# Low halves of the weight tiles: one GpSimd subtraction of 1024 columns per tile in place of two of 512

## What is computed

```
m, conv_state, s_new = token_mix(rms_norm(x), ...)      # Conformer conv group + GLA group
x = x + m
x = x + cross_attn(rms_norm(x), mk, mv, w_q, w_o)        # 4 heads, 256 memory tokens
h = rms_norm(x)
x = x + square(relu(h @ w_up)) @ w_down                  # width 4096
y = rms_norm(x)
```

## Time and profile before

| what | value |
|---|---|
| median of 3 runs | 1675.45 us (1673.5 to 1676.83) |
| profiled execution: its own time | 1673.81 us |
| profiled execution: span from first to last instruction | 1672.1 us |
| PE busy | 1511.8 us, 90% of the span |
| DVE busy | 701.2 us, 42% |
| POOL busy | 534.4 us, 32%, of which low parts 371.2 us |
| ACT busy | 461.2 us, 28% |
| mean granted TensorE clock | 0.947 |

### The profile page before, as it was taken

The page is one execution under the profiler, slowest core; times in us unless marked ns, Lnnn a source line. Parts: engine busy times, 40 slices in busy tenths (PEclk is TensorE's granted clock), DMA queues, the critical chain, the costliest instruction groups (busy, mean ns, idle before and its releaser), DMA issues.

```text
span 1672.1 us, 22350 instructions
## 1 busy us (share of the span) xinstructions
PE 1511.8 (90%) x9454; PEld 1458.9 (87%) x9454; DVE 701.2 (42%) x659; ACT 461.2 (28%) x544; POOL 534.4 (32%) x352
## 2 busy tenths in 40 slices
PE   5987777786889899997899999999999999999995
PEld 4887767776877899996699999999999999999994
DVE  6499989957861533546323221112210221112123
ACT  6422215133342323234222321112210221122211
POOL 6247759724551122210012222212212222212220
PEclk9998878988998899999899999999999999999997
DMA  6221501100020424114711111111111111111102
GB/s 228 83 71 57 62 33 57 45 26 26 14 63 29 164 94 184 51 50 152 278 38 38 51 50 51 38 51 38 51 49 50 38 50 50 50 38 50 44 31 101
DMA packets 45530, 114.00 MB, mean 68 GB/s; under 512 B 7688, under 2 KB 20248, under 8 KB 44320
## 3 DMA queue, kind: packets, MB, share of 16 engines
q1 hardware_dynamic: 43568, 104.19, 19.0%
q10 hardware_dynamic: 1904, 8.98, 1.3%
HBM read 100.85 MB, written 12.30 MB: 68 GB/s over the span
## 4 chain that ended last, share of the span: by engine, by line
PE 68%; DVE 19%; issue 6%; POOL 3%; ACT 3%; DMA 1%; DVEq 0%; SPq 0%; ACTq 0%; POOLq 0%
PE ps L978 63%; DVE conv_y L1423 10%; DVE qz L1447 1%; PE m L1049 1%; PE m L1209 1%; DVE acc L1447 1%; PE ps L1243 1%; POOL w_split L537 1%; PE m L997 1%; DVE acc L1413 1%; DMA cache_b<-in_cache_v 1%; DVE sc_t L1458 1%; DVE x_res L1821 1%; DVE tmp L1436 0%; POOL a_op L582 0%
## 5 line engine op out<-in xcount | busy, mean ns | idle before, releaser
L978 PE MATMUL ps<-a_op,w_split 128*128 128x344 f32 x4968 | 817.0, 327 | 50.8 <-DVE tmp L1491 18.7
L978 PEld LDWEIGHTS ps<-a_op,w_split 128*128 128x128 f32 x4968 | 805.6, 194 | 55.2 <-DVE tmp L1491 19.8
L537 POOL TENSOR_TENSOR w_split<-w_raw,w_split 128x512 fp32r<-128x512 f32 x250 | 371.2, 1505 | 1024.7 <-ACT w_split L624 1024.7
L978 PE MATMUL ps<-b_op,w_split 128*128 128x344 f32 x2880 | 454.6, 319 | 0.0
L978 PEld LDWEIGHTS ps<-b_op,w_split 128*128 128x128 f32 x2880 | 452.3, 188 | 0.8 <-issue 0.4
L624 ACT ACTIVATE w_split<-w_raw 128x1024 fp32r<-128x1024 f32 x125 | 131.3, 1050 | 407.3 <-PE ps L978 399.0
L1423 DVE SCALAR_TENSOR_TENSOR conv_y<-conv_in,par,conv_y 128x1024 f32<-128x1024 f32 x90 | 187.0, 2078 | 2.6
L1792 DVE SCALAR_TENSOR_TENSOR tmp<-ps,rstd 128x1032 f32<-128x1032 f32 x32 | 39.5, 1233 | 215.1 <-PE ps L978 203.2
L1802 DVE TENSOR_TENSOR x_res<-x_res,ps 128x1032 f32 x24 | 29.5, 1229 | 230.8 <-PE ps L978 230.8
L932 ACT ACTIVATE tmp<-tmp 128x1032 f32<-128x1032 f32 x32 | 34.1, 1066 | 259.1 <-DVE tmp L1792 259.1
L1632 DVE TENSOR_TENSOR x_res<-x_res,ps 128x1032 f32<-128x1032 f32 x24 | 29.5, 1229 | 166.7 <-PE ps L978 166.7
(11 more groups left out here) (205 smaller groups left out, 952.0 us busy)
## 6 DMA issues: line engine op xcount, KB each, us to landing
w_raw<-in_wt SPq DMA_DIRECT2D x125, 512.0 KB, 3.5
cache_b<-in_cache_v SPq DMA_DIRECT2D x8, 1024.0 KB, 7.3
x_in<-in_x ACTq DMA_DIRECT2D x4, 1032.0 KB, 8.1
x_spill<-x_res SPq DMA_DIRECT2D x8, 516.0 KB, 2.6
out_y<-x_res ACTq DMA_DIRECT2D x8, 516.0 KB, 3.0
cache_a<-in_cache_k SPq DMA_DIRECT2D x2, 2048.0 KB, 11.4
cache_b<-in_cache_k SPq DMA_DIRECT2D x2, 2048.0 KB, 10.4
x_res<-in_x SPq DMA_DIRECT2D x1, 3096.0 KB, 12.3
```

The lines of the kernel that those rows point to most:

```text
L537: gp.tensor_tensor(w_split[:, slot, 1, part, :], w_raw[:, slot, part, :], w_split[:, slot, 0, part, :].bitcast(F32), ALU.subtract).then_in ...
L978: last = pe.matmul(ps[:, b, 0:w], w_split[:, slot, wp, k, :], src[:, k, xp, c0:c0 + w], start=(k == 0 and j == 0), stop=(k == KT - 1 and j ...
```

## The change

POOL's low part of a tile is made by one instruction over all 8 blocks. It adds 2 to `w_low_done` when it ends, so that every count that others wait for (PE at block 0 and block 4, SP before the next load) stays as it was. PE's program isn't changed: its wait at block 0 for 2t + 1 is now met only when the whole low part is there.

```diff
@@ -532,10 +532,8 @@
             def lo(t, slot):
 
                 gp.wait_ge(w_high_done, t + 1)
-                for k in (0, KT // 2):
-                    part = slice(k, k + KT // 2)
-                    gp.tensor_tensor(w_split[:, slot, 1, part, :], w_raw[:, slot, part, :],
-                                     w_split[:, slot, 0, part, :].bitcast(F32), ALU.subtract).then_inc(w_low_done, 1)
+                gp.tensor_tensor(w_split[:, slot, 1, :, :], w_raw[:, slot, :, :],
+                                 w_split[:, slot, 0, :, :].bitcast(F32), ALU.subtract).then_inc(w_low_done, 2)
```

## The result

The changed kernel takes 1684.0 us (median of 5 runs, 1681.42 to 1685.25), the one before 1675.45. The ratio is 1.0052 with a 95% interval of 1.0037 to 1.0066: slower by 8.55 us by the medians. The forecast was slower, 1681.3 us.

The account below looks back on a forecast made before the run. PE was taken as the bound on average, DVE as the pace in the convolution. Terms 0.8 + 2.5 + 1.2 + 1.05 + 0.3 = +5.85 us on the median 1675.45 gave 1681.3 us, range 1674.5 to 1687.

Parts of the forecast that it names:

- One instruction of 2.34 us, the loads 0.19 earlier: POOL's low part: 2.34 us in place of 2.52, so SP's loads come 0.19 us earlier or more.
- Tiles 40 to 124 cost nothing: Feed-forward tiles and those before from 40: later first halves stay covered by the tile before, no cost.
- Tile 39, +1.05: PE starts tile 39 on its first half; waiting for the whole costs +1.05 us, bounds 0.9 to 1.2.
- Tiles 8, 10, 12, 20 covered (0 to +0.8): Convolution in-tiles starting later but ending before DVE reads them: counted as nothing, 0 to +0.8 us.
- The start, +0.8 (-0.7 to +1.9): Start-up: tile 0 starts 1.07 us later, 0.3 taken back through tile 5's earlier load: +0.8 us.
- The levels, +1.2: GLA levels, tiles 34 to 37: DVE's operands wait one longer POOL instruction, +1.2 us, 0 to +2.9.
- Attention, +0.3: DVE's copy of 8 columns at 751.97 us waits for the whole low part: +0.3 us, 0 to +1.1.
- The convolution, +2.5 (-4.3 to +4.6): Convolution stage: 12 disturbed low parts cost DVE's taps 0.20 us each, +2.4, plus +0.1 for tile 10.
- DVE is the pace there: Convolution stage, 76 to 332 us: DVE, busy 240 of 256 us, sets the pace rather than PE.
- nothing to measure: Rival: DVE's turns cost the same and the start gives back its 1.07; +1.5 us, 1677; chance 0.25.
- faster: Rival: DVE loses only POOL's own time, 0.19 less per low part; -3.95 us, 1671.5; chance 0.07.
- The clock: Rival: new idle times before tiles 8, 10, 39 lower PE's clock; +9 us, 1684.5, or 1686.7; chance 0.08.

Follow-up runs that it names:

- e1: Kernel before with one low subtraction per tile only for tiles 40 to 124: ratio 0.9993, -1.2 us.
- e3: Kernel before with one low subtraction only for tiles 0, 2, 3, 4, 8, 10, 12, 20 and 39: ratio 1.0009, +1.5 us.
- e6: Changed kernel with DVE's twelve short operations of the sample tokens' convolution moved behind the last tap: 1684.08 us, ratio 1.0059.
- e8: Kernel before with one low subtraction only for tiles 1, 5, 6, 7, 9, 11 and 32 to 38: ratio 1.0010, +1.7 us.
- e2: Kernel before with one low subtraction only for tiles 13 to 19 and 21 to 31: ratio 1.0037, +6.2 us.
- e4: Kernel before with POOL's tap additions split into two of 512 columns, low parts still in halves: ratio 0.9975, -4.2 us.
- f3: Kernel before with low parts in quarters of 256 columns for tiles 9 to 31, tap additions whole: ratio 0.9963, -6.2 us.
- f2: Kernel before without POOL's 30 tap additions, low parts whole for tiles 13 to 19 and 21 to 31: 1628.86 us, +5.9 over the same in halves.
- f4: Kernel before with low parts in quarters for tiles 9 to 38, whole from tile 40, tap additions in quarters of 256: ratio 0.9958, -7.0 us.

## Why the prediction was right, and where its size was off

The range and the sign held, and the sum came within 2.7 us of the medians, in part by luck: the convolution was priced too low, and the clock gave time back at tiles 37 and 53, where the sum had nothing. By its own steps:
- **One instruction of 2.34 us, the loads 0.19 earlier.** Right: 2.342 us, 125 instructions.
- **Tiles 40 to 124 cost nothing.** Right: but for tile 53 the distance between the traces is constant, and e1 is -1.2 us with an interval that holds 0.
- **Tile 39, +1.05.** Right: +1.15, at full clock, and it stays up to tile 52. At tile 53 the three traces with tile 39 whole are 1.3 us or more faster than any other, which the forecast didn't see.
- **Tiles 8, 10, 12, 20 covered (0 to +0.8).** Not borne out: e3's trace has +3.0 us between tiles 7 and 31, through the wait in front of tile 16. Tile 12 comes 4.0 us late there, of which 1.1 is from the start. DVE reads tile 12 out of PSUM 1.8 us later than before and tile 14 4.1 us later, so the lateness had reached DVE, which the step took as untouched.
- **The start, +0.8 (-0.7 to +1.9).** -0.97 in the changed kernel's profile, +1.1 in e3's and +0.8 in e6's. The waits went as told (the load's wait went and PE's took its place). The size can't be read from these: the kernels that are the same up to tile 8 differ by 3 us there, 2 of them by the clock at tile 5, which the term left out.
- **The levels, +1.2.** 1.6 us came between tiles 31 and 36, in the changed kernel's trace and in e8's. What the term left out is tile 37, where 1.8 us come back in both. So e8's +1.7 us (0.2 to 3.3 by its interval) doesn't measure this term.
- **Attention, +0.3.** It can't be told from nothing. From the end of tile 52 to the start of tile 53 PE takes 81.26 us, 80.62 before and 80.34 in e1; the other traces lie between 80.4 and 81.1.
- **The convolution, +2.5 (-4.3 to +4.6): the term that was mis-sized.** The step was "12 x 0.20", one tap more or less in a turn. The taps' own sum did what it said: 187.0 to 189.3 us, +2.3. But the stage grew by 13.1 us in that pair of traces, and e2, with 18 of its tiles whole, measures +6.2 us (+4.0 to +8.4 by its interval). Two things were left out. One is DVE's other operations, those of few columns above all, which now wait longer for POOL: +8.1 us in that trace. The other is the order in DVE's queue: a fixed number of taps stands in front of each PSUM read, and each lets one POOL instruction through, of whatever length. The longer that is, the more of POOL's work comes to stand in front of the read, where PE waits for it, and the less behind it, where DVE has time to spare. In the two places read above a mean over both sides (0.20) hides a loss of about 2 us in front, and the gain behind goes into DVE's wait for PE. That POOL's instruction size is the cause is shown by e2, e4 and f3; how the loss divides between these two ways is argued from the traces and not shown.
- **"DVE is the pace there"** was true on the average, 240 of 256 us, but in the places read above DVE and PE bound each other in turn. There, waits inside DVE count in front of the read only.

Of the rivals, "nothing to measure" and "faster" are out by the interval, the latter by the earlier trace rows's own pattern. The clock did not fall behind tiles 8, 10 and 39; where it changed, it went the other way. What stays open is how the +6 of f2 and of e2 divide over the single tiles; the executions differ there by some us for a while (e1's tile 18 comes 1.9 us later than before's, its tile 27 at the same time) though the program is the same there. And a low part that is held back until DVE's read wasn't tried.

## What to carry to other kernels

- Where GpSimd and VectorE instructions with two SBUF inputs run side by side, they take turns by whole instruction, so the size of one's instruction is its share. Cut the one off the path small (here 256 to 512 columns, -11 us), and stop before it falls behind (f4). Whether the one on the path should be large was not tried.
- Fewer instructions are worth their start-up time (here 0.19 us each on an engine with 70% idle time) only to who waits for that engine. Look first at who waits for its first half, then at who shares its port.
- A cost that evens out over a stage isn't free if it moves from behind a hand-over to in front of it. Add up each side of the hand-over by itself, and price the short operations too, not the long ones alone.
- Follow a lateness past the place where it seems covered: in e3 it was nearly gone at tiles 14 and 15 and back at tile 16.

## What had not been expected of the hardware

- DVE's work on 8 columns took 1.27 us beside POOL's 512-column and 2.38 beside its 1024-column instruction, with hardly any spread (2368 to 2382 ns over eight): a short instruction pays the full turn.
- The clock that PE is granted can differ between executions at the same tile of the same program part: tile 5 took 3.1 us in four traces and 4.7 to 5.3 in six. Two profiles can lie 2 us apart by that alone.
- It can also depend on the kernel: tile 53 took 11.5 us at full clock in the three traces with tile 39 whole, and 12.8 to 14.4 in the eleven others. A later start of one tile came with a faster one 260 us further on.
